# Delta products of one chunk alternated with inverse blocks of the next on TensorE

## The chip, the core and the metric

The kernel runs on one core of one Trainium2 chip. The metric is the device time of one execution in microseconds (us). TensorE (PE in the profile) multiplies matrices, VectorE (DVE) and ScalarE (ACT) do elementwise work and copies, GpSimd (POOL) helps with casts and rotations, and SyncE (SP) issues the large DMAs.

## The reference, cut to what matters

One encoder layer over 1024 frames of width 1024: one input projection, a sliding-window attention branch and a gated DeltaNet branch, a gated merge, an output projection, a squared-ReLU feed-forward part and two layer norms. The change lies in the DeltaNet branch, which works on chunks of 64 frames with 4 heads of width 128:

```
m_low = where(strict, (k*beta) @ k.T * decay, 0)          # 64 x 64 per head
t_inv = inverse(eye + m_low)                              # 64 x 64 per head
u = t_inv @ (v*beta);  w = t_inv @ (k*beta*exp(g))
for each chunk, in order:                                 # scan with a state per head
    v_new = u - w @ state
    o     = (q*exp(g)) @ state + a_intra @ v_new
    state = state*exp(g_last) + (k*exp(g_last-g)).T @ v_new
```

## The kernel before, in words

**Stages.** The program does the input projection, then 9 scan steps, then the branch and output projections and the feed-forward part. The change touches the scan steps alone, and TensorE's program alone.

**A step.** The 1024 frames are 8 tiles of 128 frames; a tile holds two chunks, one in partitions 0 to 63 ("low") and one in 64 to 127 ("high"). A call `step(t, a, n, ...)` works on three tiles at once: it runs the scan (and the attention) of tile t, builds the triangular inverse of tile a = t+1, and prepares tile n = t+2. The first call has no t, the last has no a; so seven calls have both.

**The inverse.** `a_kk` and `a_kq` make the products of keys and queries. `a_t1` (line 2179) transposes the first 1-I block matrix into a PSUM bank. ScalarE copies it out as `rinv`, the first version of the inverse, and signals `r0_ok`. Then come five levels of doubling: `a_y` multiplies `mm_` with `rinv`, VectorE masks the product into `ys` (`ys_ok`), and `a_u` makes one or two further products from `ys` and `tb`, which VectorE folds back into `rinv` and `tb` (`r_ok`, `tb_ok`). All of these are 64x64x64 products, one for each head and chunk. The low chunk uses the array's rows and columns 0 to 63 and the high chunk those from 64 to 127, and the two alternate in program order (`blocks`).

**The scan.** For each chunk c of tile t, `b_ks` multiplies the state, VectorE makes `xs` (`x_ok`), `b_vn` multiplies the finished inverse with `xs` (4 products of 64x64x128, all in the low quarter of the array for c = 0, all in the high quarter for c = 1). ScalarE copies the result out as `vn` (`vn_ok`), and `b_ds` and `b_o` use it. I call the products of `b_vn` the delta products.

**Fill.** `fill(f[i])` issues that many 128x128x512 products of the later projections (line 2118) at fixed points of a step. They are independent of the step's own chain and cover its waits. The list `full` says how many stand at each point; its fourth entry, between `a_t1` and `b_vn` of the first chunk, is 0.

**What sets the order.** TensorE's order is the order of the calls in `step`. An instruction carries one semaphore wait; further waits stand in front of it as instructions of TensorE's queue. `a_t1`, `a_y`, `a_u`, `b_vn` and `b_o` have a `pe.sem_inc(waited, 1)` behind their waits, an instruction that does nothing else than carry waits; the semaphore `waited` is read by nobody.

The two places that matter here are these:

```
fill(f[2]); a_t1(a); fill(f[3]); b_vn(t, 0, q); a_y(a, 1, p); fill(f[4])
...
b_scores(t, 1); b_vn(t, 1, q); a_u(a, 2, p); fill(f[8])
```

Of the kernel before, what the change touches and what calls it, by code (L numbers as in the profile page):

```python
# [37 lines left out]
NT = S // P  # L38
# [3 lines left out]
NH = 4  # L42
# [87 lines left out]
def hybrid_block(nc, A, out):  # L130
    with ExitStack() as ctx:
# [52 lines left out]
        xs = workb("xs", 512, [P, NH, P])  # L184
        vn = workb("vn", 512, [P, NH, P])
        osb = workb("osb", 512, [P, NH, P])
        ys = workb("ys", 256, [P, NH, CH])
# [12 lines left out]
        rinv, vb, kq, att, kdec = [], [], [], [], []  # L200
# [128 lines left out]
        A0, A1, T0, C0, C1, O0 = ps[2:8]  # L329
        hv = lambda bank: bank[:, :].rearrange("p (h d) -> p h d", h=NH)  # L330
        A0h, A1h, T0h, C0h, C1h, O0h = map(hv, (A0, A1, T0, C0, C1, O0))
# [1666 lines left out]
        def _(pe):  # L1998
# [135 lines left out]
                trans(C1h, lambda h: gs[p][:, G_CUM + h:G_CUM + h + 1].to_broadcast([P, P])).then_inc(grow_mm, 1)  # L2134

            def a_trq(t):
                pe.wait_ge(dn_in, 48 * t + 48)
                if not isinstance(t, int) or t >= 2:
                    pe.wait_ge(on_ok, t - 1)
                trans(C0h, lambda h: dqs[:, h, :]).then_inc(trq_mm, 1)  # L2140

            def a_trk(t, p):
                pe.wait_ge(dn_in, 48 * t + 48)
                pe.wait_ge(eg_ok, t + 1)
                trans(C1h, lambda h: dqk[p][:, NH + h, :]).then_inc(trk_mm, 1)

# [5 lines left out]
            def a_free(t):  # L2152

                if isinstance(t, int) and t == 0:
                    pe.wait_ge(uni_out, 2 * 18)
                else:
                    pe.wait_ge(a_done, t)
# [6 lines left out]
                last.then_inc(kk_mm, 1)  # L2164

            def a_kq(t, p):
                a_free(t)
                for h in range(NH):
                    for r in chunks:
                        last = mm(half(A1, 0)[r, h, :], dqk[p][:, NH + h, r], dqk[p][:, h, r], start=True, stop=True)  # L2170
                last.then_inc(kq_mm, 1)

            def a_t1(t):
                pe.wait_ge(t1_ok, t + 1)
                pe.wait_ge(m_ok, 2 * t + 2)
                pe.sem_inc(waited, 1)
                for h in range(NH):
                    for r in chunks:
                        last = mm(half(A0, 1)[r, h, :], tb[0][r, h, :], ident[r, r], start=True, stop=True)
                last.then_inc(t1_mm, 1)  # L2180
# [8 lines left out]
            def a_y(t, l, p):  # L2189

                if l == 1:
                    pe.wait_ge(m_ok, 2 * t + 2)
                    pe.wait_ge(r0_ok, t + 1)
                else:
                    pe.wait_ge(tb_ok, 4 * t + (l - 1))
                    pe.wait_ge(r_ok, 4 * t + (l - 1))
                pe.sem_inc(waited, 1)
                blocks(half(A0, 0), mm_, rinv[p]).then_inc(y_mm, 1)

            def a_u(t, l, p):  # L2200

                pe.wait_ge(ys_ok, 5 * t + l)
                if l == 1:
                    pe.wait_ge(at_ok, t + 1)
                else:
                    pe.wait_ge(tb_ok, 4 * t + (l - 1))
                pe.sem_inc(waited, 1)
                if l < 5:
                    blocks(half(A0, 0), ys, tb[(l - 1) % 2]).then_inc(ut_mm, 1)
                blocks(half(A1, 0), tb[(l - 1) % 2], ys).then_inc(u_mm, 1)  # L2210


            def b_scores(t, c):
                pe.wait_ge(rope_ok, t + 1)
                if not (isinstance(t, int) and t == 0 and c == 0):
                    pe.wait_ge(ya_ok, 2 * t + c)
                for j in range(NH):
                    last = mm(T0h[:, j, :], qb[:, c, j, :], kr[:, c * CH:c * CH + P], start=True, stop=True)
                last.then_inc(sc_mm, 1)
# [3 lines left out]
                trans(T0h, lambda j: pr[:, j, :]).then_inc(pt_mm, 1)  # L2223

            def b_pv(t, c):
                pe.wait_ge(bv_in, 32 * t + 32)
                pe.wait_ge(pt_ok, 2 * t + (c + 1))
                for e in range(2):
                    r = slice(e * HD, (e + 1) * HD)
                    last = mm(T0[r, 0:NH * CH].rearrange("p (j q) -> p j q", j=NH), vch[c][:, r], prt[:, :, r], start=True, stop=True)  # L2230
                last.then_inc(pv_mm, 1)

            def b_ks(t, c, p):

                if c == 0:
                    pe.wait_ge(qegt_ok, t + 1)
                    pe.wait_ge(ks_in, 32 * t + 32)
                    if not (isinstance(t, int) and t == NT - 1):
                        pe.wait_ge(vb_ok, t + 2)
                    if not (isinstance(t, int) and t == 0):  # L2240
                        pe.wait_ge(yd_ok, t)
                pe.wait_ge(s_ok, 2 * t + (c + 1))
                if not (isinstance(t, int) and t == 0 and c == 0):
                    pe.wait_ge(vn_ok, 2 * t + c)
                for h in range(NH):
                    last = mm((O0h, C0h)[c][:, h, :], kq[p][:, h, 2 * c:2 * c + 2, :].rearrange("p a c -> p (a c)"), st[:, h, :],
                              start=(h == 0), stop=False, skip_group_check=True)
                last.then_inc(ks_mm, 1)

            def b_vn(t, c, p):  # L2250
                r = slice(c * CH, (c + 1) * CH)
                if c == 0:
                    pe.wait_ge(a_done, t + 1)
                pe.wait_ge(x_ok, 2 * t + (c + 1))
                pe.sem_inc(waited, 1)
                for h in range(NH):
                    last = mm((C0h, C1h)[c][r, h, :], rinv[p][r, h, :], xs[r, h, :], start=True, stop=True)
                last.then_inc(vn_mm, 1)

            def b_ds(t, c, p):  # L2260
                r = slice(c * CH, (c + 1) * CH)
# [8 lines left out]
            def b_o(t, c, p):  # L2270
                r = slice(c * CH, (c + 1) * CH)
                other = slice((1 - c) * CH, (2 - c) * CH)
                pe.wait_ge(vn_ok, 2 * t + (c + 1))
                pe.sem_inc(waited, 1)
                for h in range(NH):
                    last = mm((O0h, C0h)[c][other, h, :], att[p][r, h, :], vn[r, h, :], start=False, stop=(h == NH - 1), skip_group_check=True)
                last.then_inc(o_mm, 1)
# [5 lines left out]
            def step(t, a, n, p, fill, f):  # L2283

                q = 1 - p
                fill(f[0])
                if t is not None: b_ks(t, 0, q)
                if t is not None: b_scores(t, 0)
                fill(f[1])
                if a is not None: a_kk(a, p)  # L2290
                if a is not None: a_kq(a, p)
                fill(f[2])
                if a is not None: a_t1(a)
                fill(f[3])
                if t is not None: b_vn(t, 0, q)
                if a is not None: a_y(a, 1, p)
                fill(f[4])
                if t is not None: b_ds(t, 0, q)
                fill(f[5])
                if t is not None: b_pt(t, 0)  # L2300
                if a is not None: a_u(a, 1, p)
                if t is not None: b_ks(t, 1, q)
                fill(f[6])
                if t is not None: b_pv(t, 0)
                if a is not None: a_y(a, 2, p)
                fill(f[7])
                if t is not None: b_scores(t, 1)
                if t is not None: b_vn(t, 1, q)
                if a is not None: a_u(a, 2, p)
                fill(f[8])  # L2310
                if t is not None: b_ds(t, 1, q)
                fill(f[9])
                if n is not None: a_grow(n, q)
                fill(f[10])
                if a is not None: a_y(a, 3, p)
                if t is not None: b_o(t, 0, q)
                if t is not None: b_o(t, 1, q)
                if a is not None: a_u(a, 3, p)
                fill(f[11])
                if a is not None: a_y(a, 4, p)  # L2320
                fill(f[12])
                if a is not None: a_u(a, 4, p)
                fill(f[13])
                if t is not None: b_pt(t, 1)
                if n is not None: a_trk(n, q)
                fill(f[14])
                if n is not None: a_trq(n)
                fill(f[15])
                if t is not None: b_ont(t)
                fill(f[16])  # L2330
                if a is not None: a_y(a, 5, p)
                fill(f[17])
                if t is not None: b_pv(t, 1)
                if a is not None: a_u(a, 5, p)
                fill(f[18])
                if n is not None: a_trv(n)
                fill(96)
# [228 lines left out]
```

## Time and profile before

| | |
|---|---|
| median of 3 runs | 1418.38 us (1417.59 to 1418.38) |
| the profiled execution | 1417.4 us, of it 1415.6 us span |
| TensorE busy | 1401.8 us, 99% of the span |
| its granted clock | 0.998 of full speed |
| VectorE, ScalarE, GpSimd busy | 978.6, 578.1, 276.2 us |
| one step of the scan | 46.2 us (the same group of instructions starts at 302.27 and at 348.46) |

The profiled execution lies 1.0 us below the median. In the rows, times are from the span's start. `PE` is a matmul, `PEld` the load of its weights. A matmul of the program in fp32 with 64 or 128 columns appears as two records (two passes), so the four products of `b_vn` are eight `L2257` records. A matmul's duration in a row includes its way through the array; the time that it costs in a stream is the distance from its start to the next one's.

### The profile page before, as it was taken

How to read it: one execution, taken by the hardware profiler on the slowest of the kernel's cores; microseconds unless marked ns; L12 is line 12 of the kernel's file. 1: busy time of each engine (PE TensorE's matmuls, PEld its weight loads, DVE VectorE, ACT ScalarE, POOL GpSimd, SP SyncE). 2: the span in 40 equal slices, each digit the busy share in tenths (PEclk: the TensorE clock that was granted, in tenths of full speed). 3: DMA queues.
4: the chain of work that ended last, by engine and by line, in shares of the span. 5: the costliest groups of instructions: out<-in, count | busy, mean ns of one | idle time of the engine just before them, and what ended most of it. 6: DMA issues, size and time to landing. Idle time of an engine off the chain costs nothing.

```text
span 1415.6 us, 22384 instructions
## 1 busy us (share of the span) xinstructions
PE 1401.8 (99%) x8502; PEld 1155.1 (82%) x8502; DVE 978.6 (69%) x1792; ACT 578.1 (41%) x1258; POOL 276.2 (20%) x301
## 2 busy tenths in 40 slices
PE   9999999999999999999999999999999999999997
PEld 8788887888888888778888888888888888888885
DVE  7999844666666665364528797666674777777778
ACT  5655532323332332342203355555544544444540
POOL 4332234423333243323910000000000000000002
PEclk9999999999999999999999999999999999999999
DMA  6233262443234422234442144433335975556422
GB/s 212 90 119 119 105 194 89 122 116 107 76 111 112 119 66 87 73 121 153 159 183 90 60 166 161 164 147 132 136 159 190 328 238 179 164 164 186 127 68 119
DMA packets 114134, 195.01 MB, mean 138 GB/s; under 512 B 27696, under 2 KB 59632, under 8 KB 111728
## 3 DMA queue, kind: packets, MB, share of 16 engines
q1 hardware_dynamic: 105104, 174.21, 37.1%
q10 hardware_dynamic: 8928, 19.40, 3.6%
q8 instruction: 68, 1.11, 0.3%
q14 instruction: 34, 0.28, 0.1%
HBM read 135.84 MB, written 57.74 MB: 137 GB/s over the span
## 4 chain that ended last, share of the span: by engine, by line
PE 93%; DVE 5%; DMA 1%; issue 1%; SPq 0%; ACT 0%; ACTq 0%; DVEq 0%
PE ps L2118 16%; PE ps L2500 6%; PE ps L2499 6%; PE ps L2498 6%; PE ps L2481 6%; PE ps L2482 6%; PE ps L2483 6%; PE ps L2186 4%; PE ps L2003 4%; PE ps L2004 4%; PE ps L2005 4%; PE ps L2063 3%; PE ps L2065 3%; PE ps L2064 3%; PE ps L2379 2%; PE ps L2375 2%
## 5 line engine op out<-in xcount | busy, mean ns | idle before, releaser
L2500 PE MATMUL ps<-thi,slow 128*128 128x512 f32 x416 | 162.0, 389 | 0.0
L2499 PE MATMUL ps<-tlow,shi 128*128 128x512 f32 x416 | 162.0, 389 | 0.0
L2498 PE MATMUL ps<-thi,shi 128*128 128x512 f32 x416 | 162.0, 389 | 0.0
L878 POOL TENSOR_TENSOR zt<-zt,ln2gb 128x256 f32<-128x256 f32 x4 | 3.4, 853 | 690.7 <-ACT zt L1329 690.7
L2118 PE MATMUL ps<-xh,ring2l 128*128 128x512 f32 x304 | 124.7, 410 | 0.0
L2118 PE MATMUL ps<-xl,ring2h 128*128 128x512 f32 x304 | 123.6, 407 | 0.0
L2118 PE MATMUL ps<-xh,ring2h 128*128 128x512 f32 x304 | 122.4, 403 | 0.0
L888 ACT ACTIVATE thi<-b 128x512 fp32r<-128x512 f32 x104 | 65.5, 630 | 104.2 <-PE ps L2500 103.8
L1887 DVE TENSOR_TENSOR tlow<-b,thi 128x512 fp32r<-128x512 f32 x104 | 71.9, 691 | 51.6 <-ACT thi L888 51.4
L2499 PEld LDWEIGHTS ps<-tlow,shi 128*128 128x128 f32 x416 | 78.1, 188 | 16.3
L2498 PEld LDWEIGHTS ps<-thi,shi 128*128 128x128 f32 x416 | 78.1, 188 | 16.2
L2500 PEld LDWEIGHTS ps<-thi,slow 128*128 128x128 f32 x416 | 78.1, 188 | 16.1
L777 POOL TENSOR_TENSOR ring2l<-raw,ring2h 128x256 fp32r<-128x256 f32 x112 | 88.8, 823 | 2.2
L1880 DVE TENSOR_TENSOR slow<-sraw,shi 128x512 fp32r<-128x512 f32 x104 | 71.5, 688 | 22.6 <-ACT shi L888 22.0
L888 ACT ACTIVATE shi<-sraw 128x512 fp32r<-128x512 f32 x104 | 65.0, 625 | 35.5 <-DMA zt<-xpark 18.5
L774 POOL CAST ring2h<-raw 128x1024 fp32r<-128x1024 f32 x28 | 31.3, 1117 | 229.0 <-PE ps L2118 140.6
L2118 PEld LDWEIGHTS ps<-xl,ring2h 128*128 128x128 f32 x304 | 57.2, 188 | 12.3 <-issue 0.6
L2118 PEld LDWEIGHTS ps<-xh,ring2l 128*128 128x128 f32 x304 | 57.2, 188 | 11.9 <-issue 0.6
L2118 PEld LDWEIGHTS ps<-xh,ring2h 128*128 128x128 f32 x304 | 57.3, 188 | 11.3 <-issue 0.2
L1397 DVE SCALAR_TENSOR_TENSOR cacc<-cb,convw,cacc 128x1024 f32<-128x1024 f32 x36 | 51.7, 1435 | 2.1 <-ACT cacc L959 1.2
L980 ACT ACTIVATE ub<-ps 128x512 f32<-128x512 f32 x40 | 24.0, 600 | 68.7 <-PE ps L2118 66.5
L2003 PE MATMUL ps<-slh,mg 128*128 128x512 f32 x128 | 50.0, 391 | 0.0
(442 smaller groups left out, 3638.5 us busy)
## 6 DMA issues: line engine op xcount, KB each, us to landing
raw<-in_wblk SPq DMA_DIRECT2D x55, 512.0 KB, 3.8
sraw<-hpark SPq DMA_DIRECT2D x104, 256.0 KB, 2.8
hpark<-hq SPq DMA_DIRECT2D x16, 1024.0 KB, 4.6
b<-in_wblk SPq DMA_DIRECT2D x64, 256.0 KB, 3.6
wraw<-in_wblk SPq DMA_DIRECT2D x30, 512.0 KB, 3.9
hpark<-hq SPq DMA_DIRECT2D x16, 768.0 KB, 4.9
park<-ub ACTq DMA_DIRECT2D x40, 256.0 KB, 2.2
park<-cacc ACTq DMA_DIRECT2D x12, 512.0 KB, 3.3
```

What stands on the lines that cost most here:

```text
L777: ins = pool.tensor_tensor(lo[:, k:k + 2, :], src[:, k:k + 2, :], hi[:, k:k + 2, :].bitcast(F32), ALU.subtract)
L888: cp = lambda o_, i_: act.activation(o_, i_, ACT.Copy)
L1880: tt(slow[s][:, :], sraw[s][:, :], shi[s][:, :].bitcast(F32), ALU.subtract).then_inc(lsl_ok if last else sl_ok, 1)
L1887: tt(tlow[m][:, :], src[:, :], thi[m][:, :].bitcast(F32), ALU.subtract).then_inc(ltl_ok if last else tl_ok, 1)
L2003: mm(outp, lh, rh, start=start, stop=False)
L2118: ins = mm(ps[h][:, :], w, x_, start=(r == 0), stop=(r == 23))
L2481: mm(outp, hi[:, k, :], bh_, start=first, stop=False, skip_group_check=True)
L2482: mm(outp, hi[:, k, :], bl_, start=False, stop=False, skip_group_check=True)
L2483: last = mm(outp, lo[:, k, :], bh_, start=False, stop=final, skip_group_check=True)
L2498: mm(outp, shi[s][:, ts], thi[m][:, :], start=first, stop=False, skip_group_check=True)
L2499: mm(outp, shi[s][:, ts], tlow[m][:, :], start=False, stop=False, skip_group_check=True)
L2500: return mm(outp, slow[s][:, ts], thi[m][:, :], start=False, stop=final, skip_group_check=True)
```

## The change

Three edits, all in TensorE's program.

1. `b_vn` of the first chunk and `a_y` of level 1 become one call, `vn_and_y`: each delta product, in the low quarter, is followed by a block of the high quarter; the four low blocks come afterwards. Its waits (`x_ok`, `m_ok`, `r0_ok`) all stand in front of the first product.
2. `b_vn` of the second chunk and `a_u` of level 2 become `vn_and_u` likewise, with the waits `x_ok`, `ys_ok`, `tb_ok` in front.
3. The `pe.sem_inc(waited, 1)` instructions are taken out, and with them the waits that an earlier wait of the same queue already covers.

The first and the last call of `step`, which lack a or t, keep the old order for these products.

```diff
@@ a_t1, a_y, a_u, b_o (shown together)
             def a_t1(t):
                 pe.wait_ge(t1_ok, t + 1)
-                pe.wait_ge(m_ok, 2 * t + 2)
-                pe.sem_inc(waited, 1)
...
                 else:
-                    pe.wait_ge(tb_ok, 4 * t + (l - 1))
                     pe.wait_ge(r_ok, 4 * t + (l - 1))
-                pe.sem_inc(waited, 1)
                 blocks(half(A0, 0), mm_, rinv[p]).then_inc(y_mm, 1)
...
                     pe.wait_ge(tb_ok, 4 * t + (l - 1))
-                pe.sem_inc(waited, 1)
                 if l < 5:
...
             def b_vn(t, c, p):
-                if c == 0:
+                if c == 0 and t == NT - 1:
                     pe.wait_ge(a_done, t + 1)
                 pe.wait_ge(x_ok, 2 * t + (c + 1))
-                pe.sem_inc(waited, 1)
...
+            def vn_and_y(t, a, p):
+
+                q = 1 - p
+                pe.wait_ge(x_ok, 2 * t + 1)
+                pe.wait_ge(m_ok, 2 * a + 2)
+                pe.wait_ge(r0_ok, a + 1)
+                low, high = chunks
+                for h in range(NH):
+                    last = mm(C0h[low, h, :], rinv[q][low, h, :], xs[low, h, :], start=True, stop=True)
+                    if h == NH - 1:
+                        last.then_inc(vn_mm, 1)
+                    mm(half(A0, 0)[high, h, :], mm_[high, h, :], rinv[p][high, h, :], start=True, stop=True)
+                for h in range(NH):
+                    last = mm(half(A0, 0)[low, h, :], mm_[low, h, :], rinv[p][low, h, :], start=True, stop=True)
+                last.then_inc(y_mm, 1)
+
+            def vn_and_u(t, a, p):
+
+                q = 1 - p
+                pe.wait_ge(x_ok, 2 * t + 2)
+                pe.wait_ge(ys_ok, 5 * a + 2)
+                pe.wait_ge(tb_ok, 4 * a + 1)
+                low, high = chunks
+                for h in range(NH):
+                    last = mm(C1h[high, h, :], rinv[q][high, h, :], xs[high, h, :], start=True, stop=True)
+                    if h == NH - 1:
+                        last.then_inc(vn_mm, 1)
+                    mm(half(A0, 0)[low, h, :], ys[low, h, :], tb[1][low, h, :], start=True, stop=True)
+                    mm(half(A1, 0)[low, h, :], tb[1][low, h, :], ys[low, h, :], start=True, stop=True)
+                for h in range(NH):
+                    last = mm(half(A0, 0)[high, h, :], ys[high, h, :], tb[1][high, h, :], start=True, stop=True)
+                last.then_inc(ut_mm, 1)
+                for h in range(NH):
+                    last = mm(half(A1, 0)[high, h, :], tb[1][high, h, :], ys[high, h, :], start=True, stop=True)
+                last.then_inc(u_mm, 1)
...
             def b_o(t, c, p):
-                pe.wait_ge(vn_ok, 2 * t + (c + 1))
-                pe.sem_inc(waited, 1)
...
                 fill(f[3])
-                if t is not None: b_vn(t, 0, q)
-                if a is not None: a_y(a, 1, p)
+                if t is not None and a is not None:
+                    vn_and_y(t, a, p)
+                elif t is not None:
+                    b_vn(t, 0, q)
+                else:
+                    a_y(a, 1, p)
```

Waits that an earlier one covers are also dropped in `a_trq`, `a_trk`, `a_kq`, `b_scores`, `b_pv` and `b_ks`. No other engine's program changes.

On TensorE, around the first delta products of a step that has both t and a, before (`L2179` is `a_t1`, `L2257` the delta products, `L2186` the blocks of `a_y`, `L2118` fill, `L2267` is `b_ds`):

```order
L2179 MATMUL ps<-cst,tb_106 64x64 [waits t1_ok,m_ok]
L2179 MATMUL ps<-cst,tb_106 64x64 x7
L2257 MATMUL ps<-xs,rinv_89 64x128 [waits a_done,x_ok]
L2257 MATMUL ps<-xs,rinv_89 64x128 x3
L2186 MATMUL ps<-rinv_84,mm 64x64 [waits m_ok,r0_ok]
L2186 MATMUL ps<-rinv_84,mm 64x64 x7
L2118 MATMUL ps<-xh,ring2l_290 128x512
```

and the same place now:

```order
L2178 MATMUL ps<-cst,tb_106 64x64 [waits t1_ok]
L2178 MATMUL ps<-cst,tb_106 64x64 x7
L2263 MATMUL ps<-xs,rinv_89 64x128 [waits r0_ok,m_ok,x_ok]
L2266 MATMUL ps<-rinv_84,mm 64x64
L2263 MATMUL ps<-xs,rinv_89 64x128
L2266 MATMUL ps<-rinv_84,mm 64x64
L2263 MATMUL ps<-xs,rinv_89 64x128
L2266 MATMUL ps<-rinv_84,mm 64x64
L2263 MATMUL ps<-xs,rinv_89 64x128
L2266 MATMUL ps<-rinv_84,mm 64x64
L2268 MATMUL ps<-rinv_84,mm 64x64 x4
```

The number of products is the same. The wait on `r0_ok` has moved from behind the four delta products to ahead of them.

On TensorE, around the second delta products, before (`L2218` is `b_scores`):

```order
L2218 MATMUL ps<-kr,qb 128x128 x3
L2257 MATMUL ps<-xs,rinv_89 64x128 [waits x_ok]
L2257 MATMUL ps<-xs,rinv_89 64x128 x3
L2186 MATMUL ps<-tb_107,ys 64x64 [waits ys_ok,tb_ok]
L2186 MATMUL ps<-tb_107,ys 64x64 x7
L2186 MATMUL ps<-ys,tb_107 64x64 x8
L2267 MATMUL ps<-vn,kdec_93 128x128 [waits vn_ok]
```

and now:

```order
L2215 MATMUL ps<-kr,qb 128x128 x3
L2279 MATMUL ps<-xs,rinv_89 64x128 [waits tb_ok,ys_ok,x_ok]
L2282 MATMUL ps<-tb_107,ys 64x64
L2283 MATMUL ps<-ys,tb_107 64x64
...
L2285 MATMUL ps<-tb_107,ys 64x64 x4
L2288 MATMUL ps<-ys,tb_107 64x64 x4
L2298 MATMUL ps<-vn,kdec_93 128x128 [waits vn_ok]
```

Here too the count is the same, and the waits on `ys_ok` and `tb_ok` have moved ahead of the delta products. The three lines of one head stand four times where "..." is.

## Rows read from the trace of the kernel before

**Rows 1.** The page: busy time, granted clock, chain by engine.
```profile
PE 1401.8 (99%) x8502; PEld 1155.1 (82%) x8502; DVE 978.6 (69%) x1792; ACT 578.1 (41%) x1258; POOL 276.2 (20%) x301
...
PEclk9999999999999999999999999999999999999999
...
PE 93%; DVE 5%; DMA 1%; issue 1%; SPq 0%; ACT 0%; ACTq 0%; DVEq 0%
```

**Rows 2.** Windows in the scan: width, busy by engine, clock, DMA share, GB/s.
```profile
302.00:348.00 46.00, 46.00 (x485) 37.52 (x484) 30.53 (x89) 14.74 (x65) 15.65 (x19) 1.00 0.36 103
```

**Rows 3.** Timeline, first delta products: start, us, engine, instruction, idle before and releaser.
```profile
347.91 0.39 PE L2118 MATMUL ps<-xh,ring2h 128*128 128x512 f32 x1
348.13 0.40 PE L2118 MATMUL ps<-xl,ring2h 128*128 128x512 f32 x1
348.46 0.68 PE L2179 MATMUL ps<-cst,tb 64*64 64x64 f32 x16
348.97 0.93 PE L2257 MATMUL ps<-xs,rinv 64*64 64x128 f32 x7
349.19 0.38 ACT L888 ACTIVATE rinv<-ps 128x256 f32<-128x256 f32 x1 [6.87 <-PE ps L2179]
349.68 0.27 PE L2186 MATMUL ps<-rinv,mm 64*64 64x64 f32 x1
349.74 0.27 PE L2257 MATMUL ps<-xs,rinv 64*64 64x128 f32 x1
349.78 0.69 PE L2186 MATMUL ps<-rinv,mm 64*64 64x64 f32 x15
350.05 0.59 ACT L888 ACTIVATE vn<-ps 64x512 f32<-64x512 f32 x1 [0.48 <-PE ps L2257]
350.40 0.50 PE L2118 MATMUL ps<-xh,ring2l 128*128 128x512 f32 x1
```

**Rows 4.** ScalarE's instructions on `rinv`: count, durations, and what ended its idle time.
```profile
L888 ACT ACTIVATE rinv<-ps x8: 383/383/384, 220.4 to 533.9; 128x256 f32<-128x256 f32 x8
its engine sat idle before it (us, times) until:
  PE ps L2179: 57.0, 8
```

**Rows 5.** Timeline of PE, second delta products.
```profile
314.26 0.76 PE L2257 MATMUL ps<-xs,rinv 64*64 64x128 f32 x5
314.76 0.27 PE L2186 MATMUL ps<-tb,ys 64*64 64x64 f32 x1
314.86 0.27 PE L2257 MATMUL ps<-xs,rinv 64*64 64x128 f32 x1
...
314.97 0.27 PE L2257 MATMUL ps<-xs,rinv 64*64 64x128 f32 x1
...
315.08 0.27 PE L2257 MATMUL ps<-xs,rinv 64*64 64x128 f32 x1
...
315.48 0.22 PE L2186 MATMUL ps<-ys,tb 64*64 64x64 f32 x1
315.48 0.22 PE L2186 MATMUL ps<-tb,ys 64*64 64x64 f32 x1
315.53 0.22 PE L2186 MATMUL ps<-ys,tb 64*64 64x64 f32 x1
...
315.65 0.63 PE L2186 MATMUL ps<-ys,tb 64*64 64x64 f32 x13
316.21 0.37 PE L2267 MATMUL ps<-vn,kdec 64*128 64x128 f32 x1
```

**Rows 6.** Timeline of VectorE and ScalarE beside the second delta products.
```profile
312.66 0.37 DVE L1603 SCALAR_TENSOR_TENSOR xs<-ps,gs,vb 64x128 f32<-64x128 f32 x1
...
313.06 0.42 DVE L1567 TENSOR_TENSOR ys<-ps,cst 128x256 f32<-128x256 f32 x1
...
315.38 0.59 ACT L888 ACTIVATE vn<-ps 64x512 f32<-64x512 f32 x1 [2.55 <-PE ps L2257]
```

**Rows 7.** Timeline of PE, from fill to `a_kk`, which has no idle instruction.
```profile
345.46 0.40 PE L2118 MATMUL ps<-xl,ring2h 128*128 128x512 f32 x1
345.79 0.69 PE L2163 MATMUL ps<-dqk 128*64 128x64 f32 x16
```

More of the change, by code:

```diff
@@ L2136, in a_trq @@
             def a_trq(t):
-                pe.wait_ge(dn_in, 48 * t + 48)
+                if t == 0:
+                    pe.wait_ge(dn_in, 48 * t + 48)
                 if not isinstance(t, int) or t >= 2:
@@ L2142, in a_trk @@
             def a_trk(t, p):
-                pe.wait_ge(dn_in, 48 * t + 48)
+                if t > 0:
+                    pe.wait_ge(dn_in, 48 * t + 48)
                 pe.wait_ge(eg_ok, t + 1)
@@ L2166, in a_kq @@
             def a_kq(t, p):
-                a_free(t)
                 for h in range(NH):
@@ L2213, in b_scores @@
             def b_scores(t, c):
-                pe.wait_ge(rope_ok, t + 1)
+                if c == 0:
+                    pe.wait_ge(rope_ok, t + 1)
                 if not (isinstance(t, int) and t == 0 and c == 0):
@@ L2225, in b_pv @@
             def b_pv(t, c):
-                pe.wait_ge(bv_in, 32 * t + 32)
+                if c == 0:
+                    pe.wait_ge(bv_in, 32 * t + 32)
                 pe.wait_ge(pt_ok, 2 * t + (c + 1))
@@ L2242, in b_ks @@
                 pe.wait_ge(s_ok, 2 * t + (c + 1))
-                if not (isinstance(t, int) and t == 0 and c == 0):
-                    pe.wait_ge(vn_ok, 2 * t + c)
                 for h in range(NH):
@@ L2307, in step @@
                 if t is not None: b_scores(t, 1)
-                if t is not None: b_vn(t, 1, q)
-                if a is not None: a_u(a, 2, p)
+                if t is not None and a is not None:
+                    vn_and_u(t, a, p)
+                elif t is not None:
+                    b_vn(t, 1, q)
+                else:
+                    a_u(a, 2, p)
                 fill(f[8])
```

## The prediction

> **What bounds the kernel now.** I read the page first. TensorE is busy for 99% of the span at full granted clock and makes 93% of the chain that ended last [rows 1]. Then I cut the scan into windows as long as a step: in one of 46 us TensorE is busy for all 46.00, while VectorE has 30.53 and ScalarE 14.74 [rows 2]. So every wait inside a step is covered at present, and the time of a step is the sum of what stands in TensorE's queue. Two conclusions follow. A removed wait or idle instruction gives time back only where a hole of TensorE goes with it, and there is none that the windows show. And a wait that becomes visible is paid in full, for no slack stands behind it. Last I read the timelines at the two places where instructions move [rows 3, 5, 6], and asked of each wait what ends it and what covers it.
>
> **Where the seven joint steps differ.** Only the calls of step with both t and a use the new orders: seven of them. All terms below are per step, times seven.
>
> **Term 1, the wait for rinv, which is now ahead of the delta products.** Before, a_t1 starts at 348.46, and the first delta product right behind it at 348.97. ScalarE takes up the copy of a_t1's result at 349.19 and needs 0.38, to 349.57. The first product of a_y starts at 349.68, 0.11 later; that is the delay of a signal and of the start [rows 3]. Between 348.97 and 349.68 TensorE isn't idle: it runs seven of the eight passes of the delta products. They are the cover of this wait, and the fill count at this point is 0. In the changed order the first delta product itself waits for r0_ok. So it can't start before 349.68: a hole of 349.68 - 348.97 = 0.71 us. Nothing in the queue can step in, for all that stands behind the waiting instruction (delta products, blocks, fill) stands behind it in the same queue. Nor can the copy come sooner. ScalarE was idle for 6.87 us before it and was released by a_t1 itself, and a_t1 runs as early as before (term 4). This holds in each step: the copy has the same duration, 383 to 384 ns, all 8 times, and ScalarE always sat idle until a_t1 released it [rows 4].
>
> A group that starts into an empty part of the array also starts slower. Seven distances between eight delta passes take 315.08 - 314.26 = 0.82 us behind the scores [rows 5], but 349.74 - 348.97 = 0.77 where they follow a_t1 in the same quarter [rows 3]: 0.05 more. Term 1 is 0.71 + 0.05 = 0.76 us, times 7 = +5.3 us. Its bounds: if the signal took no time at all, the hole would end with the copy at 349.57, 0.60 a step or +4.2; above, +5.6 if the restart costs 0.09 rather than 0.05.
>
> **Term 2, the alternation in vn_and_y.** Here I ask what each quarter of the array has to do. A delta pass takes 0.109 us: (315.08 - 314.86) / 2 = 0.11, and 0.77 / 7 = 0.11 [rows 3, 5]. A pass of a 64-column block takes about 0.055 to 0.058 in its quarter: 315.53 - 315.48 = 0.05, and from 315.65 to 316.21 the last of them run in one quarter alone at that pace [rows 5]. The low quarter has eight delta passes and eight block passes, 0.87 + 0.46 = 1.33 us, in the old order and in the new. Before, the high blocks already run beside it: the first starts at 349.68, ahead of the last delta pass at 349.74, though it is behind it in the queue [rows 3]. The old order ends from 348.97 to 350.40, 1.43 with the turn to the fill, which is that 1.33 and 0.10 for the turn. Alternating therefore has nothing left to hide in this group. Term 2 is 0.
>
> **Term 3, vn_and_u.** The high quarter has eight delta passes and 16 block passes: 0.87 + 0.93 = 1.80 us. The old order takes 316.21 - 314.26 = 1.95, again 1.80 and the turn of 0.1 to 0.15 [rows 5]. There the low blocks began at 314.76, beside the fifth or sixth of the delta passes. The new order can't be shorter than its high quarter, 1.80. It can be longer if the high quarter has to keep step with the low: a head has four low passes, 4 x 0.058 = 0.234, for two delta passes, 0.218; 0.016 for each of four heads is 0.06 a step. I take 0, with +0.4 us over seven steps as the upper bound. The waits ahead of it cost nothing: xs is ready at 312.66 + 0.37 = 313.03, ys at 313.06 + 0.42 = 313.48 [rows 6], and tb of level 1 must be there already for the a_y of level 2, which stands ahead of the scores and waits for it in the code before. The delta products start at 314.26 [rows 5]. The cover is the fill product and the scores; without them it would be a hole of up to 0.4. Next in line is b_ds at 316.21, which waits for ScalarE's vn, done at 315.38 + 0.59 = 315.97 [rows 5, 6]. That leaves 0.24 us; a signal later by 0.06 stays under it. In the first group the copy of vn is done at 350.64 [rows 3] with three fill products behind the group, and it moves with the group.
>
> **Term 4, idle instructions and covered waits.** A joint step has 15 calls with such an instruction (a_t1, five a_y, five a_u, two b_vn, two b_o). What one costs is seen from two transitions of the same kind. From a fill product to a_t1, which has one, is 348.46 - 348.13 = 0.33 us [rows 3]. From a fill product to a_kk, which has none, is 345.79 - 345.46 = 0.33 [rows 7]. The difference is 0.00, so the queue reads ahead far enough to hide them. From above: fill to fill is 348.13 - 347.91 = 0.22 [rows 3], so at most the 0.11 that a turn takes beyond that could be due to it; 15 x 0.11 x 7 = 11.6 us. From below it costs nothing or, if an instruction less lets the queue run differently, some hundredths. I take 0, by the nearest row, a_kk. The dropped waits are of the same sort: each is on a value that the queue has already waited for.
>
> **Sum.** 5.3 + 0 + 0 + 0 = +5.3 us. On the profiled execution's own time, 1417.4, this is 1422.7. That execution is 1.0 us below the median of the runs, 1418.38, so for a median the sum gives 1423.7. Since that execution and the lowest run, 1417.59, are close, I say 1423.5. After the scan, TensorE stays the bound (the chain has 5% of VectorE, at the end of the program), so what a step loses isn't given back later.
>
> **A rule weighed.** In the trace, 64 more moving columns cost 0.109 - 0.058 = 0.051 us a pass, so of the 0.109 of a delta pass only 0.007 isn't streaming. The weight loads of passes that follow each other in one quarter are hidden already. The Trainium skill ("TensorE: Matmul & The Clock Gate", Part 3, The mechanism) says that a weight load overlaps with running matmuls only when the row group differs. By that rule the old order would pay for each of 16 delta passes a load that alternating hides; at the page's columns/1.2, an estimate of 53 ns, this is 16 x 0.053 x 7 = 6 us, and the change would come out at about 1417.5. The trace disagrees with the rule's "only".
>
> **The rivals.**
>
> A (forecast): the hole of 0.76 appears, the rest is nothing. 1423.5; own range 1422.0 (bound of 0.60) to 1425.0 (0.80 a step, +0.4 from term 3, and the spread of the runs). Chance 84%.
>
> B: the alternation hides weight loads. From rows its ceiling is that a whole block pass, 0.058, is the load: 16 x 0.058 x 7 = 6.5 us, 1417.0. For it: the eight passes do stand in one quarter. Against it: the 0.007 above. Chance 3%.
>
> C (the other side): the idle instructions are on TensorE's path. At the ceiling, 11.6 us, the result is 1423.5 - 11.6 = 1411.9. It decides from 5.3 / (15 x 7) = 0.05 us for each; at just that it would be 1418.2. For it: 105 instructions are many, and every turn takes 0.11 more than a fill. Against it: a_kk's turn takes as much without one. Chance 7%: 4 for faster, 3 for within 0.2%.
>
> D: the quarters don't run side by side in the new order. Then vn_and_y takes 8 x 0.109 + 16 x 0.058 = 1.80 instead of 1.33, and vn_and_u 0.87 + 0.93 + 0.93 = 2.73 instead of 1.80: 1.40 x 7 = 9.8 more, 1433. For it: the new order alternates two lengths of pass. Against it: at 314.76 and 314.86 just these two lengths run beside each other [rows 5]. Chance 4%.
>
> E: the wait isn't met as I think: r0_ok comes early enough that the hole is under half of mine, below 1421. That would need a_t1 earlier, and the rows leave no way. Chance 2%.
>
> **How the numbers follow.** What this kernel's measurement can tell from no change is about 0.2%, 2.8 us. Slower by more than that: A and D, 0.88. Within: B, E and 3 of C's 7, 0.08. Faster: the other 4 of C, 0.04. The range is A's own, stretched downward to take in part of C and E and upward for runs that lie high: 1420.5 to 1426.0; it leaves out D, and most of B and C.
>
> **What would show it.** Right: in the timeline after, the delta products (line 2263) start about 0.11 us behind the end of ScalarE's copy into rinv, TensorE has an idle gap of 0.4 to 0.7 us before them, named as a wait for ACT rinv, seven times; the step grows from 46.2 to about 46.9; the groups from first delta pass to the next fill keep 1.4 to 1.5 and 1.95. Wrong: a step of 46.2 or less, a group shorter than 1.33 or 1.80, a turn from fill into a_t1 or a_y below 0.33, or low and high passes that start one after another.

## The result, and the profile after

The changed kernel takes 1423.55 us (median of 7 runs, 1422.93 to 1423.86). The kernel before takes 1418.28 us in the same comparison (7 runs, 1417.53 to 1418.65). The difference is +5.27 us, a ratio of 1.0035 with a 95% interval of 1.0026 to 1.0045: slower, as forecast. The predicted time was 1423.5.

The page of the kernel after, the lines that answer to [rows 1]:

```profile
span 1421.1 us, 22276 instructions
...
PE 1402.6 (99%) x8502; PEld 1154.1 (81%) x8502; DVE 977.5 (69%) x1792; ACT 578.1 (41%) x1258; POOL 277.5 (20%) x301
...
PEclk9999999999999999999999999999999999999999
...
PE 93%; DVE 5%; DMA 1%; issue 1%; SPq 0%; ACT 0%; ACTq 0%; DVEq 0%
```

The busy time of TensorE hardly moved (1401.8 to 1402.6) while the span grew by 5.5 us, at the same clock. So the new time is idle time. The page is too coarse to show where; the same window as in [rows 2] isn't:

```profile
302.00:348.00 46.00, 45.42 (x472) 36.79 (x472) 29.85 (x87) 14.78 (x65) 15.64 (x19) 1.00 0.36 101
```

TensorE now rests for 0.58 of 46 us. The list of waits of TensorE over the joint steps (what waited, for whom, us in total, times, longest) has one line; before, it has none:

```profile
PE ps L2263 <- ACT rinv L888: 4.0, 7, 0.6
```

Seven waits, one in each joint step, of the first delta product (line 2263) for ScalarE's copy into `rinv`. The timeline at that place answers to [rows 3]:

```profile
303.12 0.68 PE L2178 MATMUL ps<-cst,tb 64*64 64x64 f32 x16
303.85 0.39 ACT L888 ACTIVATE rinv<-ps 128x256 f32<-128x256 f32 x1 [6.87 <-PE ps L2178]
304.38 0.29 PE L2263 MATMUL ps<-xs,rinv 64*64 64x128 f32 x1 [0.58 <-ACT rinv L888]
304.38 0.33 PE L2266 MATMUL ps<-rinv,mm 64*64 64x64 f32 x2
304.51 0.27 PE L2263 MATMUL ps<-xs,rinv 64*64 64x128 f32 x1
...
305.05 0.38 PE L2263 MATMUL ps<-xs,rinv 64*64 64x128 f32 x2
...
305.27 0.62 PE L2268 MATMUL ps<-rinv,mm 64*64 64x64 f32 x8
305.83 0.50 PE L2118 MATMUL ps<-xh,ring2l 128*128 128x512 f32 x1
```

From the start of `a_t1` to the first delta product it is 304.38 - 303.12 = 1.26 us; before it was 348.97 - 348.46 = 0.51 [rows 3]. The difference is 0.75 in these rounded rows and 0.74 without rounding. The 0.58 in the bracket is less than that because the page counts the last passes of `a_t1` as busy until they have left the array. Two more rows of the same timeline, further on, give the length of a step:

```profile
307.80 0.50 PE L2118 MATMUL ps<-xh,ring2l 128*128 128x512 f32 x1
...
310.70 0.27 PE L2126 MATMUL ps<-cst,pr 128*128 128x128 f32 x1
...
350.08 0.39 PE L2178 MATMUL ps<-cst,tb 64*64 64x64 f32 x6
```

A step is 350.08 - 303.12 = 46.96 us, where it was 348.46 - 302.27 = 46.19 (46.18 in the middle of the seven joint steps). And the second delta products, answering to [rows 5]:

```profile
315.91 0.32 PE L2279 MATMUL ps<-xs,rinv 64*64 64x128 f32 x1
315.92 0.33 PE L2282 MATMUL ps<-tb,ys 64*64 64x64 f32 x2
316.07 0.27 PE L2279 MATMUL ps<-xs,rinv 64*64 64x128 f32 x1
316.08 0.28 PE L2283 MATMUL ps<-ys,tb 64*64 64x64 f32 x2
316.18 0.27 PE L2279 MATMUL ps<-xs,rinv 64*64 64x128 f32 x1
...
316.89 0.57 PE L2285 MATMUL ps<-tb,ys 64*64 64x64 f32 x7
317.30 0.63 PE L2288 MATMUL ps<-ys,tb 64*64 64x64 f32 x8
317.86 0.60 PE L2298 MATMUL ps<-vn,kdec 64*128 64x128 f32 x3
```

The delta passes (2279) run in one quarter, behind the first every 0.11 us, the low blocks beside them. From the first to `b_ds` it is 317.86 - 315.91 = 1.95 us, to the hundredth what it was before, and there is no wait ahead of them.

### The profile page after: what moved, and what is told of

It is laid out like the page before. It is cut to its first block, busy times and chain, and to the rows that moved or that the text cites. A ratio compares the mean times of both kernels' runs of the same rounds, so it can differ in the third digit from the quotient of the medians.

```text
span 1421.1 us, 22276 instructions
## 1 busy us (share of the span) xinstructions
PE 1402.6 (99%) x8502; PEld 1154.1 (81%) x8502; DVE 977.5 (69%) x1792; ACT 578.1 (41%) x1258; POOL 277.5 (20%) x301
## 4 chain that ended last, share of the span: by engine, by line
PE 93%; DVE 5%; DMA 1%; issue 1%; SPq 0%; ACT 0%; ACTq 0%; DVEq 0%
PE ps L2118 16%; PE ps L2536 6%; PE ps L2535 6%; PE ps L2537 6%; PE ps L2520 6%; PE ps L2519 6%; PE ps L2518 6%; PE ps L2003 4%; PE ps L2005 4%; PE ps L2004 4%; PE ps L2185 3%; PE ps L2063 3%; PE ps L2065 3%; PE ps L2064 3%; PE ps L2416 2%; PE ps L2412 2%
## 5 line engine op out<-in xcount | busy, mean ns | idle before, releaser
L2118 PE MATMUL ps<-xh,ring2l 128*128 128x512 f32 x304 | 124.6, 410 | 0.0
L2118 PE MATMUL ps<-xl,ring2h 128*128 128x512 f32 x304 | 123.5, 406 | 0.0
L2118 PE MATMUL ps<-xh,ring2h 128*128 128x512 f32 x304 | 122.5, 403 | 0.0
L2118 PEld LDWEIGHTS ps<-xl,ring2h 128*128 128x128 f32 x304 | 57.1, 188 | 12.4 <-issue 0.6
L2118 PEld LDWEIGHTS ps<-xh,ring2l 128*128 128x128 f32 x304 | 57.1, 188 | 12.1 <-issue 0.6
L2118 PEld LDWEIGHTS ps<-xh,ring2h 128*128 128x128 f32 x304 | 57.2, 188 | 11.4 <-issue 0.2
```

Of the source, the lines that this page charges most:

```text
L2118: ins = mm(ps[h][:, :], w, x_, start=(r == 0), stop=(r == 23))
```

## The experiments

Theory A: the wait for `rinv`, moved ahead of the delta products that had covered it, is the whole loss. The rivals: part of it comes from `vn_and_u` (F), alternation makes passes slower (D), idle instructions cost time and their removal hid part of the loss (C). The table has all runs; "step" is the time from one start of `a_t1` to the next in the middle of the scan, read in each timeline. The ratio is to the kernel before, run on the same chip.

| kernel | median us (runs) | before us | ratio (95%) | step us |
|---|---|---|---|---|
| before | | 1418.28 | | 46.18 |
| changed | 1423.55 (7) | 1418.28 | 1.0035 (1.0026 to 1.0045) | 46.96 |
| first pair undone | 1418.07 (11) | 1417.93 | 1.0001 (0.9992 to 1.0010) | 46.16 |
| first pair alone | 1423.27 (5) | 1417.93 | 1.0035 (1.0022 to 1.0049) | 46.94 |
| edit 3 alone | 1417.69 (11) | 1417.93 | 0.9999 (0.9990 to 1.0008) | 46.16 |
| idle instructions four times | 1425.13 (5) | 1417.93 | 1.0053 (1.0039 to 1.0066) | 47.16 |
| fill in the hole | 1420.33 (11) | 1418.05 | 1.0014 (1.0005 to 1.0023) | 46.51 |
| copy behind another | 1425.06 (5) | 1418.05 | 1.0049 (1.0036 to 1.0062) | 47.23 |
| wait behind three heads | 1419.37 (12) | 1418.05 | 1.0009 (1.0000 to 1.0018) | 46.37 |
| two turns less | 1416.89 (12) | 1418.05 | 0.9991 (0.9983 to 1.0000) | 46.00 |
| one turn less | 1416.59 (11) | 1417.97 | 0.9991 (0.9982 to 1.0000) | 46.00 |

### First pair undone

```diff
-                if t is not None and a is not None:
-                    vn_and_y(t, a, p)
-                elif t is not None:
-                    b_vn(t, 0, q)
-                else:
-                    a_y(a, 1, p)
+                if t is not None: b_vn(t, 0, q)
+                if a is not None: a_y(a, 1, p)
```

(on the changed kernel)

> The changed kernel with vn_and_y undone: the first delta products stand ahead of a_y of level 1 again, and the wait on r0_ok behind them. vn_and_u and edit 3 stay. Theory A (the exposed wait for ScalarE's copy into rinv is the whole loss): the hole of 0.74 us a step goes, 7 x 0.76 = 5.3 us come back, so 1418.3 us, a ratio to before of 1.000. Theory F (the loss comes from vn_and_u too, since the high quarter has to keep step with the low): 0.06 x 7 = 0.4 us stay, 1418.7. Theory D (alternation makes the passes slower in both groups): well over half of the 5.3 would stay, 1421 or more.

Measured: 1418.07, ratio 1.0001. The loss is gone, and TensorE's wait for `rinv` is no longer in its list. In the timeline of this kernel the copy again lies beside the delta passes:

```profile
303.12 0.68 PE L2178 MATMUL ps<-cst,tb 64*64 64x64 f32 x16
303.64 0.93 PE L2252 MATMUL ps<-xs,rinv 64*64 64x128 f32 x7
303.85 0.39 ACT L888 ACTIVATE rinv<-ps 128x256 f32<-128x256 f32 x1 [6.86 <-PE ps L2178]
304.39 0.27 PE L2185 MATMUL ps<-rinv,mm 64*64 64x64 f32 x1
```

Here `vn_and_u` is still the new one. The step is 46.16 us, the same as that of the kernel with edit 3 alone, where it is the old one. So `vn_and_u` costs and gains nothing: F falls, and D with it for this group. (The median here is 0.38 us above that of edit 3 alone, about F's size, but the steps are equal and the 0.45 us between the two traces is there already at the first `a_t1`, ahead of the first joint step.) For `vn_and_y` D is answered by the run with fill in the hole.

### First pair alone

```diff
-                if t is not None: b_vn(t, 0, q)
-                if a is not None: a_y(a, 1, p)
+                if t is not None and a is not None:
+                    vn_and_y(t, a, p)
+                elif t is not None:
+                    b_vn(t, 0, q)
+                else:
+                    a_y(a, 1, p)
```

(on the kernel before, `vn_and_y` as in the change)

> The kernel before with vn_and_y alone: no vn_and_u, all idle instructions and covered waits kept. Theory A: the whole loss is here, 1418.3 + 5.3 = 1423.6 us, ratio 1.0037, with a hole of 0.58 us (as the trace counts idle time) before each of seven first delta products. Theory C (the idle instructions cost time, and the changed kernel gained by losing them): this kernel would be slower than the changed one, by up to the same amount, so above 1424.5.

Measured: 1423.27, ratio 1.0035, the changed kernel's own. A step is 0.76 us longer than before. Its list of waits has the line again, under its own number:

```profile
PE ps L2268 <- ACT rinv L888: 4.0, 7, 0.6
```

### Edit 3 alone

Both calls of `step` in the old order, the idle instructions and covered waits out as in the change.

> The kernel before with edit 3 alone (the idle instructions and covered waits out), both groups in the old order. Theory A: nothing, 1418.3 us, within 0.3. Theory C: each of 15 idle instructions a step gives back some hundredths of a us; at 0.01 each it would be 1.1 us, 1417.2, at 0.05 each 5.3 us, 1413.

Measured: 1417.69, ratio 0.9999 (0.9990 to 1.0008). The step is shorter by 0.02 us, which over seven steps is 0.14 us and can't be told from nothing in the times. The traces place those 0.02: the run `a_y` of level 3, `b_o`, `b_o`, `a_u` of level 3 is shorter by that much, 2.36 us instead of 2.38; no other group differs by 0.01.

### Idle instructions four times

```diff
-                pe.sem_inc(waited, 1)
+                for _ in range(4):
+                    pe.sem_inc(waited, 1)
```

(at all five places of TensorE's program, on the kernel before)

> The kernel before with each of TensorE's idle instructions issued four times (45 more in a joint step, some 350 in all). Theory A (the queue reads ahead far enough to hide them): 1418.3 us, within 0.5. Theory C: each costs its own time on the path; at 0.05 us each that is 2.3 us a step, 18 us in all, 1436. In between: the queue's lead is used up at some of the 15 places, where the group ahead is short, and a few us are lost.

Measured: 1425.13, +7.2 us, neither A's 1418.3 nor C's 1436, but the case between. The timeline of this kernel at the first delta products:

```profile
303.95 0.68 PE L2180 MATMUL ps<-cst,tb 64*64 64x64 f32 x16
304.53 1.05 PE L2261 MATMUL ps<-xs,rinv 64*64 64x128 f32 x8
304.68 0.38 ACT L888 ACTIVATE rinv<-ps 128x256 f32<-128x256 f32 x1 [6.87 <-PE ps L2180]
305.61 0.68 PE L2187 MATMUL ps<-rinv,mm 64*64 64x64 f32 x16
...
306.22 0.50 PE L2118 MATMUL ps<-xh,ring2l 128*128 128x512 f32 x1
```

and at the run of `a_y`, `b_o`, `b_o`, `a_u`:

```profile
322.94 0.68 PE L2187 MATMUL ps<-rinv,mm 64*64 64x64 f32 x16
323.52 1.55 PE L2281 MATMUL ps<-vn,att 64*64 64x128 f32 x15
...
325.97 0.50 PE L2118 MATMUL ps<-xl,ring2h 128*128 128x512 f32 x1
```

The first group takes 306.22 - 303.95 = 2.27 us against 350.40 - 348.46 = 1.94 before [rows 3]: 0.33 more. Six more instructions stand inside it, those of `b_vn` and `a_y` (those of `a_t1` stand ahead of its start). The blocks no longer start ahead of the last delta pass. The second takes 3.03 us; in the kernel before the same run takes 2.38:

```profile
320.94 0.51 PE L2186 MATMUL ps<-rinv,mm 64*64 64x64 f32 x10
321.23 0.32 PE L2276 MATMUL ps<-vn,att 64*64 64x128 f32 x1
...
323.32 0.50 PE L2118 MATMUL ps<-xl,ring2h 128*128 128x512 f32 x1
```

That is 0.65 more, with nine more instructions inside it, those of `b_o`, `b_o` and `a_u`. The trace also records the idle instructions themselves, here those of `b_vn` (shortest, median and longest duration in ns):

```profile
L2259 PEldq EVENT_SEMAPHORE  x64: 51/51/369, 256.9 to 591.5; - x64
```

An idle instruction takes 0.051 us by itself, and the next one mostly starts 0.15 us after it. So three more take 0.45 us of TensorE's queue, not the 0.05 each of C. This can be followed at `a_y`: its first block starts 305.61 - (304.68 + 0.38) = 0.55 us behind the end of the copy, where it was 0.11 before [rows 3], and 0.11 + 3 x 0.15 is 0.56. How much of that is seen in the length of a group depends on what the array still has to do meanwhile: 0.33 of 0.9 us in the first group, 0.65 of 1.4 in the second. At the ten other calls of a step, 30 more instructions cost nothing, 4.5 us of the queue's time; that holds for the second `b_vn` and `a_u` of level 2 too, which stand behind other small groups without fill (the stretch from the scores to the fill behind `b_ds` is 4.01 us in both kernels). So neither A's reason nor C's holds everywhere: the time is there, the queue's lead hides it at most places, and at the count that the kernel had it hid all but 0.02 us of it. What sets the lead at each place wasn't tested.

### Fill in the hole

```diff
-            full = [12, 2, 6, 0, 3, 12, 0, 1, 0, 11, 2, 9, 11, 2, 11, 0, 2, 4, 1]
+            full = [12, 2, 6, 3, 3, 12, 0, 1, 0, 11, 2, 9, 11, 2, 11, 0, 2, 4, 1]
```

(on the changed kernel)

> The changed kernel with three fill products between a_t1 and vn_and_y (the fourth entry of full is 3 instead of 0; the three are missing from the fill at the end of the step). Theory A: the hole of 0.74 us is covered, but the queue turns from small products to fill and back once more. From the trace of the changed kernel, a small group, six fill products and a small group take 0.15 + 1.26 + 0.33 = 1.74 from last start to first start, so three take about 1.05, where the fill itself is worth 3 x 0.227 = 0.68 and the direct step 0.05: 0.32 a step is lost against the kernel before instead of 0.76. With seven or eight steps this gives 1418.3 + 2.3 to 2.6 = 1420.6 to 1420.9, some 2.8 us below the changed kernel. If turns were free: 1418.3. If the hole weren't the cause: 1423.5 or 1426.

Measured: 1420.33, +2.3 us over before, 0.3 below the range that was expected. The timeline of this kernel:

```profile
304.93 0.68 PE L2178 MATMUL ps<-cst,tb 64*64 64x64 f32 x16
305.54 0.50 PE L2118 MATMUL ps<-xh,ring2l 128*128 128x512 f32 x1
305.66 0.38 ACT L888 ACTIVATE rinv<-ps 128x256 f32<-128x256 f32 x1 [6.87 <-PE ps L2178]
305.87 0.39 PE L2118 MATMUL ps<-xh,ring2h 128*128 128x512 f32 x1
306.11 0.40 PE L2118 MATMUL ps<-xl,ring2h 128*128 128x512 f32 x1
306.43 0.32 PE L2263 MATMUL ps<-xs,rinv 64*64 64x128 f32 x1
```

The wait is covered, and of the loss of 5.3 us three are back. What stays, 46.51 - 46.16 = 0.35 us a step, is the way from small products to fill and back: 306.43 - 304.93 = 1.50 us from `a_t1` to the delta products, of which 0.51 is the direct way and 0.68 the fill's own worth; the rest is 0.31. The other 0.05 is in the group behind: from the first delta pass to the next fill product it takes 1.48 us instead of 1.43, all of the difference ahead of the second delta pass. The alternation is all there in this kernel, and behind that second pass it costs nothing, so D falls for `vn_and_y` too.

### Copy behind another

```diff
+                cp(sqj[:, 0:NH, 0:CH], half(A0, 1))
                 cp(rinv[p][:, :, :], half(A0, 1)).then_inc(r0_ok, 1)
```

(in ScalarE's program, on the changed kernel)

> The changed kernel with a second, idle copy of the same size on ScalarE ahead of the one into rinv, so that r0_ok comes later by one copy's issue. Nothing else reads it. Theory A: the hole grows by what the copy is late, 0.27 to 0.38 us (the copy takes 0.38 in the trace, two in a row on ScalarE may overlap by some tenths), times 7 = 1.9 to 2.7 us: 1425.4 to 1426.3. If the wait for rinv weren't what holds TensorE there, the time would stay at 1423.5.

Measured: 1425.06, +1.5 us over the changed kernel's 1423.55, which was measured in another comparison; by the ratios 1.0049 to 1.0035, +2.0; by the steps 7 x 0.27 = 1.9. Expected were 1.9 to 2.7, 1425.4 at the least. The timeline of this kernel:

```profile
304.38 0.38 ACT L888 ACTIVATE sqj<-ps 128x256 f32<-128x256 f32 x1 [6.86 <-PE ps L2179]
304.66 0.38 ACT L888 ACTIVATE rinv<-ps 128x256 f32<-128x256 f32 x1
305.18 0.29 PE L2264 MATMUL ps<-xs,rinv 64*64 64x128 f32 x1 [0.85 <-ACT rinv L888]
```

The copy into `rinv` starts 0.28 us later than it would (304.66 instead of 304.38), the idle time before the delta product goes from 0.58 to 0.85, and the step from 46.96 to 47.23. TensorE follows ScalarE one to one: this is the run that names the wait.

### Wait behind three heads

```diff
-                pe.wait_ge(m_ok, 2 * a + 2)
-                pe.wait_ge(r0_ok, a + 1)
                 low, high = chunks
+                for h in range(NH - 1):
+                    mm(C0h[low, h, :], rinv[q][low, h, :], xs[low, h, :], start=True, stop=True)
+                pe.wait_ge(m_ok, 2 * a + 2)
+                pe.wait_ge(r0_ok, a + 1)
                 for h in range(NH):
...
                     mm(half(A0, 0)[high, h, :], mm_[high, h, :], rinv[p][high, h, :], start=True, stop=True)
+                    if h == 0:
+                        mm(C0h[low, NH - 1, :], rinv[q][low, NH - 1, :], xs[low, NH - 1, :], start=True, stop=True).then_inc(vn_mm, 1)
```

(on the changed kernel; the delta product inside the loop goes)

> The changed kernel with the delta products of three heads ahead of the waits on m_ok and r0_ok; behind these the high blocks, with the fourth delta product behind the first of them, then the low blocks. Theory A: six delta passes (0.65 us) run in the wait of 0.74. What is left is at most 0.1 a step, so 1418.3 + 0 to 0.8 = 1418.3 to 1419.1. This keeps work of both quarters alternating only at one place; if the alternation itself were what costs, it would recover just as well, so this run tells only whether the place of the wait is enough; with the run that has the first pair alone it gives both sides.

Measured: 1419.37, a little outside what was expected (0 to 0.8 us lost; 1.3 lost). The timeline of this kernel:

```profile
348.87 0.82 PE L2261 MATMUL ps<-xs,rinv 64*64 64x128 f32 x6
349.08 0.39 ACT L888 ACTIVATE rinv<-ps 128x256 f32<-128x256 f32 x1 [6.87 <-PE ps L2178]
349.61 0.24 PE L2265 MATMUL ps<-rinv,mm 64*64 64x64 f32 x1
349.62 0.32 PE L2267 MATMUL ps<-xs,rinv 64*64 64x128 f32 x1
...
349.77 0.27 PE L2267 MATMUL ps<-xs,rinv 64*64 64x128 f32 x1
```

Three heads ahead of the wait bring most of the loss back, which again says that the place of the wait decides. I had counted the remaining gap (six passes end 0.09 us before 349.61) and forgotten the restart: the last head's two passes are 0.15 apart instead of 0.11. These 0.09 and 0.05, and another 0.03 behind the last delta pass, are the 0.18 by which the group is longer than in the kernel with edit 3 alone. Even the fourth head is needed as cover.

### Two turns less, and one

```diff
-            full = [12, 2, 6, 0, 3, 12, 0, 1, 0, 11, 2, 9, 11, 2, 11, 0, 2, 4, 1]
+            full = [12, 2, 6, 0, 3, 12, 0, 0, 0, 12, 2, 9, 11, 2, 11, 0, 6, 0, 1]
```

(on the kernel with edit 3 alone)

> The old order with edit 3, and the fill put at other places: the single fill product between a_y of level 2 and the second scores goes to the fill before a_grow, and the four between a_y of level 5 and the last b_pv go to the fill before a_y of level 5. It is a try at a version that beats both kernels, from the finding that a turn from small products to fill and back costs 0.1 to 0.3 us. Expected if all waits at these places stay covered: 0.08 + 0.15 us a step, times 8, 1418.3 - 1.8 = 1416.5. If ys of level 5 comes too late for the last a_u (ready about 0.76 us after the last a_y pass starts, needed after about 0.75): 0 to 0.2 a step is lost again, 1416.5 to 1418.3. If the scores wait for ScalarE's y: slower than 1418.3.

Measured: 1416.89, ratio 0.9991 (0.9983 to 1.0000). The step is 46.00 us, 0.16 shorter than with edit 3 alone instead of the 0.23 that was expected, and the list `full` is used in seven steps, not eight: 7 x 0.16 = 1.1 us. The second run keeps only the later of the two moves:

```diff
-            full = [12, 2, 6, 0, 3, 12, 0, 1, 0, 11, 2, 9, 11, 2, 11, 0, 2, 4, 1]
+            full = [12, 2, 6, 0, 3, 12, 0, 1, 0, 11, 2, 9, 11, 2, 11, 0, 6, 0, 1]
```

> The old order with edit 3 and one move of fill alone: the four fill products between a_y of level 5 and the last b_pv go to the fill before a_y of level 5. In the run with both moves a step took 46.00 us instead of 46.16, and by its trace the whole gain of 0.20 lies at this place, while the single fill product moved from before the second scores gave nothing (8.24 us with it, 8.01 and the 0.23 of the fill without) and the fill products elsewhere took 0.04 more. If the gain is this turn's alone: 45.96 to 46.00 us a step, 1418.1 - 1.1 to 1.5 = 1416.6 to 1417.0, ratio 0.9990 to 0.9993. If the two moves gained together: 1417.3 or more.

Measured: 1416.59, ratio 0.9991 (0.9982 to 1.0000), the same step of 46.00. By the steps the gain is this turn's alone. The timeline of the kernel with two turns less, where the blocks of level 5, `b_pv` and the last `a_u` now follow each other:

```profile
336.58 0.68 PE L2185 MATMUL ps<-rinv,mm 64*64 64x64 f32 x16
337.19 0.65 PE L2228 MATMUL ps<-prt,vch 128*64 128x256 f32 x4
337.79 0.68 PE L2185 MATMUL ps<-ys,tb 64*64 64x64 f32 x16
```

Both versions lie 1.2 to 1.4 us below the kernel before, with an interval that just touches no change; two independent comparisons agree. They are also some 6.5 us below the changed kernel (5.3 and 1.2 to 1.4).

## Why the prediction was right

**Term 1, the wait for rinv (+0.76 a step, +5.3).** Right. Start to start, `a_t1` to delta product grew by 0.74 us, and the group behind it, 304.38 to 305.83, is 1.45 us where it was 1.43. The sum is 0.76. The split was off: a hole of 0.71 and a restart of 0.05 were forecast, 0.74 and 0.02 came (the 0.09 of the upper bound came from no row). In the new order it is 0.14 from the end of the copy (303.85 + 0.39) to the first delta product, not 0.11. That isn't because the array stood idle: with the first pair undone the first block of `a_y` joins running delta passes and still starts 304.39 - (303.85 + 0.39) = 0.15 behind the copy, and the kernel with edit 3 alone has the same 0.15. The 0.11 belongs to the kernel before, where an idle instruction stands in front of the waiting product; each kernel without one there whose product waits for the copy has 0.14 or 0.15. In the old order the 0.04 between them is hidden, for the low quarter ends the group: it takes 1.43 us with and without it. In the new order it would be part of the hole, but no run has `vn_and_y` with an idle instruction in front, so that isn't shown. That this term is the whole loss is shown twice, by undoing it and by making it alone; that it is this wait, by making the copy late, and by covering it with fill.

**Term 2, alternation in vn_and_y (0).** Right. What a quarter has to do stays, and the high blocks ran beside the last delta passes already; behind the first, the delta passes stay 0.109 us apart.

**Term 3, vn_and_u (0, at most +0.4).** Right at 0: 1.95 us before and after, and equal steps with and without it (46.16). The upper bound didn't come about, since the high quarter's passes stayed at 0.11 and didn't wait for the low ones.

**Term 4, idle instructions (0).** Right as a size; 0.02 us a step came back. The reason was too simple: the row that I went by was a turn from fill, where the queue has read ahead. An idle instruction does take the queue's time, 0.15 us where several follow each other, and in two groups, which hold five of the fifteen calls, the lead is too small to hide three more at each. At the count that the kernel had this was nearly hidden.

**The sum.** For the two profiled executions: 7 x (0.76 - 0.02) = 5.2 of 5.5 us. The rest is 7 x 0.04: in the changed kernel the twelve fill products after the first `b_ds` take 310.70 - 307.80 = 2.90 us, and in the kernel with edit 3 alone 2.86. The kernels with a late copy and with three heads ahead show the same 0.04, those with the first pair undone or alone don't. I didn't try to find its cause. The forecast's nearness to the measured median, 1423.5 against 1423.55, is luck in part: the 0.02 of term 4 and these 0.04 have opposite signs, the hole's 0.03 too little and the restart's 0.03 too much cancel, and 1423.5 was a choice between the sum's 1422.7 and 1423.7. Good to a few tenths of a us is what the terms can claim.

**The rule that was weighed.** The delta passes stand 0.109 us apart in one quarter alone and 0.109 to 0.110 alternated with the other quarter's. Had alternating row groups hidden weight loads, the second would be shorter. B is out.

## What to carry to other kernels

Joining two groups of products into one moves their waits to the front of the first. Before doing it, ask for each wait what ran while it was outstanding; if that is the group which now stands behind it, the wait is paid in full, here 0.74 us for the sake of an overlap that already existed. And count the work of each quarter of the array before alternating: if the busiest quarter has the same work in both orders, there is nothing to gain.

## What the runs showed of the hardware that I had not expected

- TensorE starts a product of an idle quarter ahead of older ones of a busy quarter: the first block at 349.68, the last delta pass at 349.74 [rows 3]. So program order didn't have to alternate for the quarters to overlap.
- Instructions that only wait or signal take TensorE's queue 0.15 us each where they follow each other. What shows of it depends on the queue's lead: 30 more a step for nothing, 6 more for 0.33 us in one group and 9 more for 0.65 in another.
- From the end of ScalarE's copy to the start of the product that waits for it, it is 0.11 us when an idle instruction carries the wait and 0.14 to 0.15 when none stands there, whether TensorE was running (0.15, first pair undone) or idle (0.14, changed kernel).
- A turn from 64-wide products to three 512-wide ones and back costs 0.31 us over the fill's own 0.68.
